# Six sums over the channels as two fp32r matmuls each, in the second mixer of a two-block network

## What is computed

```
qf = jax.nn.silu(q.astype(jnp.float32))
f = lower_bound + (1 - lower_bound) * jax.nn.sigmoid(f_logit.astype(jnp.float32))
kf = 1 - f
...
diff = b_[:, :, :, None, :] - b_[:, :, None, :, :]
decay = jnp.exp(jnp.where(causal[:, :, None], diff, -jnp.inf))
scores = jnp.einsum('bhtk,bhtsk,bhsk->bhts', q_, decay, k_)
o_intra = jnp.einsum('bhts,bhsv->bhtv', scores, v_)
```

## Time and profile before

| | |
|---|---|
| time, median of 3 runs (lowest to highest) | 1392.86 us (1390.56 to 1392.98) |
| the profiled execution's own time | 1392.87 us |
| its span | 1391.0 us |
| granted TensorE clock, mean | 0.999 of full speed |
| TensorE matmul (PE) busy | 1377.5 us, 99% |
| TensorE weight load (PEld) busy | 1147.1 us, 82% |
| VectorE (DVE) busy | 775.9 us, 56% |
| ScalarE (ACT) busy | 598.9 us, 43% |
| GpSimd (POOL) busy | 594.9 us, 43% |
| mean DMA rate | 105 GB/s |

### The profile page before, as it was taken

One profiled execution on the slowest core, in us unless ns is written; L12 is line 12 of the kernel. 1 busy time (PEld: TensorE's weight loads), 2 busy tenths in 40 slices (PEclk: granted clock), 3 DMA queues, 4 the chain that ended last, 5 costly groups with the idle time before them and its releaser, 6 DMA issues.

```text
span 1391.0 us, 20905 instructions
## 1 busy us (share of the span) xinstructions
PE 1377.5 (99%) x7666; PEld 1147.1 (82%) x7666; DVE 775.9 (56%) x1524; ACT 598.9 (43%) x1030; POOL 594.9 (43%) x314
## 2 busy tenths in 40 slices
PE   8999999999999999999999999999999999999998
PEld 7877777778998888888889978878898888888887
DVE  5897865456677666666884878522563323231222
ACT  7223555464255445443222525575354444342222
POOL 7432222216244444444543479523345444444441
PEclk9999999999999999999999999999999999999999
DMA  7931111015525444445662241121213233222321
GB/s 219 218 92 61 31 62 46 19 44 167 167 77 181 136 138 151 150 131 161 202 209 83 65 117 61 31 61 31 92 61 121 90 102 110 90 87 87 106 84 61
DMA packets 188309, 146.15 MB, mean 105 GB/s; under 512 B 21561, under 2 KB 186659, under 8 KB 188240
## 3 DMA queue, kind: packets, MB, share of 16 engines
q1 hardware_dynamic: 186528, 144.59, 33.9%
q10 hardware_dynamic: 1200, 0.36, 0.1%
q0 software_dynamic: 512, 0.25, 0.1%
HBM read 143.08 MB, written 2.10 MB: 104 GB/s over the span
## 4 chain that ended last, share of the span: by engine, by line
PE 91%; DVE 5%; DMA 2%; issue 1%; ACT 0%; DVEq 0%; ACTq 0%
PE ps L2120 27%; PE ps L2121 26%; PE ps L2122 26%; DMA ada<-in_ada_w 2%; DVE ps L1736 2%; PE ps L2564 2%; PE ps L2308 2%; PE ps L2391 1%; PE ps L2374 1%; PE ps L2621 1%; PE ps L2591 1%; PE ps L2644 1%; PE ps L2656 1%; PE ps L2206 0%; PE ps L2388 0%
## 5 line engine op out<-in xcount | busy, mean ns | idle before, releaser
L778 POOL TENSOR_TENSOR w_lo<-raw,w_hi 128x1024 fp32r<-128x1024 f32 (+2 forms) x224 | 515.5, 2305 | 726.4 <-ACT w_hi L843 448.5
L2120 PE MATMUL ps<-h_hi,w_hi 128*128 128x512 f32 (+1 forms) x1336 | 505.2, 378 | 0.6 <-DVE h_lo L1371 0.6
L2121 PE MATMUL ps<-h_lo,w_hi 128*128 128x512 f32 (+1 forms) x1336 | 494.3, 370 | 0.0
L2122 PE MATMUL ps<-h_hi,w_lo 128*128 128x512 f32 (+1 forms) x1336 | 494.2, 370 | 0.0
L2120 PEld LDWEIGHTS ps<-h_hi,w_hi 128*128 128x128 f32 x1336 | 252.3, 189 | 60.5 <-issue 17.7
L2122 PEld LDWEIGHTS ps<-h_hi,w_lo 128*128 128x128 f32 x1336 | 252.2, 189 | 43.2
L2121 PEld LDWEIGHTS ps<-h_lo,w_hi 128*128 128x128 f32 x1336 | 252.6, 189 | 39.9 <-issue 0.5
L843 ACT ACTIVATE w_hi<-raw 128x1024 fp32r<-128x1024 f32 (+2 forms) x136 | 133.6, 984 | 265.5 <-PE ps L2122 256.4
L1111 ACT ACTIVATE w_hi<-raw 128x1024 fp32r<-128x1024 f32 x88 | 93.2, 1059 | 218.0 <-PE ps L2122 218.0
L2120 PE MATMUL ps<-g_hi,w_hi 128*128 128x512 f32 (+1 forms) x394 | 146.8, 373 | 0.0
L2121 PE MATMUL ps<-g_lo,w_hi 128*128 128x512 f32 (+1 forms) x394 | 144.7, 367 | 0.0
(11 more groups left out here) (364 smaller groups left out, 1707.8 us busy)
## 6 DMA issues: line engine op xcount, KB each, us to landing
ada<-in_ada_w SPq DMA_DIRECT2D x48, 512.0 KB, 3.8
raw<-in_ffn_w_up SPq DMA_DIRECT2D x22, 1024.0 KB, 5.0
raw<-in_w_up SPq DMA_DIRECT2D x22, 1024.0 KB, 4.9
raw<-in_w_in SPq DMA_DIRECT2D x21, 1024.0 KB, 5.1
raw<-in_ffn_w_down SPq DMA_DIRECT2D x8, 896.0 KB, 5.7
raw<-in_w_down SPq DMA_DIRECT2D x8, 896.0 KB, 4.7
raw<-in_w_in SPq DMA_DIRECT2D x16, 256.0 KB, 3.8
raw<-in_w_out SPq DMA_DIRECT2D x4, 1024.0 KB, 5.1
```

The lines of the kernel that those rows point to most:

```text
L778: pool.tensor_tensor(w_lo[slot % 4][:, 0:nk, :], part[:, :, slot % 2 * P:(slot % 2 + 1) * P], w_hi[slot % 4][:, 0:nk, :].bitcast(F32), ALU ...
L2120: pe.matmul(out_ap, w, x, start=first, stop=False, **kw)
L2121: pe.matmul(out_ap, w, xl, start=False, stop=False, **kw)
L2122: return pe.matmul(out_ap, wl, x, start=False, stop=last, **kw)
```

## The change

The products of the summed chunks go to PSUM banks 4 and 5 in place of `hn`. ScalarE copies each to an fp32r tile, `sum_hi`; VectorE subtracts that from the product into `sum_lo`; TensorE sums both with the matrix of ones read as fp32r, one matmul after the other into the same bank. The semaphore of the low part takes the place of `multiplied` on TensorE. It and that of the high part are those which the first block's convolution used, under new names, counted on from 4 (`CC`). `sum_hi` lies in room behind `kd_odd` in the tile `off`, `sum_lo` where `hn` is.

```diff
+        sum_hi = sb("sum_hi", [P, 2, T], F32R, at=off_at + 4 * HG * T)
+        sum_lo = sb("sum_lo", [P, 2, T], F32R, at=hn_at)
+        PRODUCT_BANK = [4, 5]
...
                 hi(s + 4)
+                if S_QH + 2 < s < S_PAIRED:
+                    for c in ((0, 1), (2, 3), (4, 5))[s - S_KV2 + 1]:
+                        act.wait_ge(multiplied, c + 1)
+                        act.activation(sum_hi[:, c % 2, :], ps[PRODUCT_BANK[c % 2]][:, :], ACT.Copy).then_inc(split_hi_done, 1)
...
-                out = hn[:, c % 2, :]
+                out = ps[PRODUCT_BANK[c % 2]][:, :]
...
+            def product_lo(c):
+                dve.wait_ge(split_hi_done, CC + c + 1)
+                dve.tensor_tensor(sum_lo[:, c % 2, :], ps[PRODUCT_BANK[c % 2]][:, :], sum_hi[:, c % 2, :].bitcast(F32),
+                                  ALU.subtract).then_inc(split_lo_done, 1)
...
             scale_queries(0)
+            product_lo(0)
+            product_lo(1)
...
                     if c + 2 < SUMMED_CHUNKS:
                         multiply(c + 2)
+                for c in EARLY_CHUNKS[s]:
+                    if c + 2 < SUMMED_CHUNKS:
+                        product_lo(c + 2)
...
                 if c < SUMMED_CHUNKS:
-                    pe.wait_ge(multiplied, c + 1)
-                    ins = pe.matmul(bank[:, :], ones[:, :], hn[:, c % 2, :], start=True, stop=True)
+                    pe.wait_ge(split_lo_done, CC + c + 1)
+                    pe.matmul(bank[:, :], ones[:, :].bitcast(F32R), sum_hi[:, c % 2, :], start=True, stop=False)
+                    ins = pe.matmul(bank[:, :], ones[:, :].bitcast(F32R), sum_lo[:, c % 2, :], start=False, stop=True)
```

More of the change, by code:

```diff
@@ L199, in build @@
         sq = sb("sq", [P, 2, T])
+        hn_at = offset[0]
         hn = sb("hn", [P, 2, T])
@@ L333, in build @@
         pv_done, o_copied = sem("pv_done"), sem("o_copied")
-        tap_done, acc_added, ln_sum, ln_centred, ln_sq, ln_sqsum, ln_root, ln_norm, cv_ready, cv_hi_done, cv_lo_done = (
+        tap_done, acc_added, ln_sum, ln_centred, ln_sq, ln_sqsum, ln_root, ln_norm, cv_ready, split_hi_done, split_lo_done = (
             sem("tap_done"), sem("acc_added"), sem("ln_sum"), sem("ln_centred"), sem("ln_sq"), sem("ln_sqsum"), sem("ln_root"),
-            sem("ln_norm"), sem("cv_ready"), sem("cv_hi_done"), sem("cv_lo_done"))
+            sem("ln_norm"), sem("cv_ready"), sem("conv_and_sums_hi_done"), sem("conv_and_sums_lo_done"))
         att_hi_done, att_lo_done = sem("att_hi_done"), sem("att_lo_done")
@@ L1080, in _ @@
                 act.wait_ge(cv_ready, c + 1)
-                act.activation(cv_hi[:, c, :], acc[:, c, :], ACT.Copy).then_inc(cv_hi_done, 1)
+                act.activation(cv_hi[:, c, :], acc[:, c, :], ACT.Copy).then_inc(split_hi_done, 1)
                 hi(S_ATTN + 6 + c)
@@ L1697, in _ @@
             for c in range(CC):
-                dve.wait_ge(cv_hi_done, c + 1)
+                dve.wait_ge(split_hi_done, c + 1)
                 dve.tensor_tensor(cv_lo[:, c, :], acc[:, c, :], cv_hi[:, c, :].bitcast(F32),
-                                  ALU.subtract).then_inc(cv_lo_done, 1)
+                                  ALU.subtract).then_inc(split_lo_done, 1)
                 gated_attention(4 + c)
@@ L2414, in _ @@
             for s in range(S_CONV, S_OUT):
-                tile(s, cv_hi, cv_lo, ready=parts(cv_lo_done) if s == S_CONV else None)
+                tile(s, cv_hi, cv_lo, ready=parts(split_lo_done) if s == S_CONV else None)
             def ada_tile(n, buf, count):
```

## The result

| | before | after |
|---|---|---|
| time, median of 20 runs each (lowest to highest) | 1393.13 us (1390.56 to 1395.13) | 1390.21 us (1387.77 to 1392.58) |
| the profiled execution's own time | 1392.87 us | 1389.30 us |
| its span | 1391.0 us | 1387.6 us |
| matmul (PE) busy | 1377.5 us | 1374.2 us |
| VectorE (DVE) busy | 775.9 us | 780.2 us |

The ratio after to before is 0.9981, with a 95% interval of 0.9976 to 0.9987: 1.8 to 3.3 us less. 1.6 us were forecast (1391.3 us, range 1389.5 to 1393.3), from a median of three runs that lay 0.3 us lower.

A forecast was written before the change was run, and what follows sets the result against it. TensorE's matmuls were taken to bound the kernel (under way for 99% of the span), unless TensorE then waits for VectorE and GpSimd. 2.42 - 0.48 - 0.35 = 1.6 us saved, giving 1391.3 us, range 1389.5 to 1393.3.

The forecast's parts named there:

- TensorE's own saving: Six fp32 sums, 5.14 us, become twelve fp32r matmuls, 2.72 us: 2.42 us saved, 0.81 a pair.
- Chunks 0 and 1: First pair of sums: subtractions end near 819.5, TensorE wants them at 820.82, so no wait, 1.3 us spare.
- Chunks 2 and 3: Second pair of sums: chunk 3's product, still held by GpSimd's `kd_odd`, makes TensorE wait; 0.48 us lost.
- Chunks 4 and 5: Third pair of sums: no TensorE wait, but `merge_decays(0)` 0.28 us later; 1.94 us saved at the attention's first products.
- Steps 0 to 2: Attention steps: `merge_decays(1)` gets its turn one `lo` sooner, step 1's scores end near 846.0; just fits.
- The rival in which VectorE stays: Steps 0 to 2: `merge_decays(1)` waits for the next `lo` as before; 0 to 0.6 us remains, 1392.6 us; chance 0.19.
- Chunk 10: Level 3's queries and keys both end near 857.9, chunk 10 starts near 858.1; 0.35 us lost, 1.6 left.
- all of it is kept: Rival: both half-microsecond waits, at chunk 3 and chunk 10, are absent; 1390.45 us; chance 0.18.
- the likeliest case: The forecast itself, 1.6 us saved, 1391.3 us, own range 1390.7 to 1392.0; chance 0.52.
- Slower by a turn: Rival at level 3: `scale_queries(3)` loses one more turn, ends at 861.4; 1.9 us slower, 1394.8 us; chance 0.07.
- No fp32r rate: Rival at the sums: twelve matmuls cost 0.857 us each, as in fp32; 5.1 us more, 1398 us; chance 0.02.

The follow-up runs named there:

- run 9: Changed kernel with `kd_odd` behind chunk 3's product, GpSimd's low weights a level later, chunk 6's scores behind step 1's; ratio to before 0.9983, median 1389.82 us.
- Run 2: Changed kernel with the products kept in `hn` in SBUF instead of PSUM; one execution, 1393.60 us, lead -2.20 us after chunk 10.
- run 3: Changed kernel with GpSimd's first `kd_odd` made to wait for the product of chunk 3; ratio to before 0.9970, 1388.98 us.
- run 7: Changed kernel with the edits of run 3 and run 6 together; ratio to before 0.9986, 1390.58 us.
- run 6: Changed kernel with GpSimd's low weights of tiles 140 and 141 each made one level later; one execution, 1391.44 us, lead 1.95 us after chunk 10.

## Why the prediction was right, point by point

- **TensorE's own saving, 2.42 us.** Right, and 0.11 us too small. The pairs cost 0.91 us, and run 9, where nothing waits, keeps 2.53. The other 0.1 lies in the tiles behind the first two pairs, 0.05 in each: tile 135 took 5.50 us behind the fp32 sums (822.53, where they end, to 828.03) and takes 5.44 behind the new ones (821.60 to 827.04), because the first matmuls behind an fp32 sum start about 0.232 us apart (seven steps from 822.76 to 824.39).
- **Chunks 0 and 1, no wait.** Right: the subtractions end at 819.2, 1.5 us before TensorE wants them. Run 2 shows that this hung on the operand in PSUM: held by GpSimd, they start chunk 1 2.5 us later (8.39 us behind tile 134's start in place of 5.90), and a stretch at the lower clock follows.
- **Chunks 2 and 3, 0.48 us lost.** Right in place and cause, 0.61 measured: 0.56 up to the next tile, and 0.05 in that tile, whose first matmuls start about 0.232 us apart, as they do behind an fp32 sum. The product of chunk 3 took 2.69 us with its output in PSUM, so the place of the output frees nothing; run 3 took `kd_odd` out of its way and the wait went. Chunk 3 itself started at 828.11 on the clock of the kernel before (0.13 is added from here on to times of the changed kernel), where 828.15 was forecast. What the count left out is that a stalled pair does not run at 0.227 us: its second matmul starts 0.30 behind the first (827.98 to 828.28).
- **Chunks 4 and 5, VectorE 0.28 us later.** Right in kind: `merge_decays(0)` starts at 831.80, which is 831.93 on the clock of the kernel before, 0.41 later. The lead at step 0 is 1.91 against 1.94.
- **Steps 0 to 2, VectorE comes forward by one turn.** Right. `merge_decays(1)` was there at 838.1 (837.8 by the count), went ahead of the second `lo`, and step 1's scores ended at 846.16 (846.0). TensorE passed with the lead unchanged at 1.93. The rival in which VectorE stays would have shown 0 to 0.6. How tight it is appears in run 7: 0.6 us more lead, and 0.32 of it is lost at that very place.
- **Chunk 10, 0.35 us lost.** Right in place, but mis-sized: 0.14 measured, 0.06 at its start and 0.08 within it. `kd_odd` ended at 857.67, not 857.9, and chunk 10 started 0.15 behind that, not 0.2. The queries were not the limit: `scale_queries(3)` ended at 855.44, where the count had both near 857.9. VectorE had waited 1.38 us for GpSimd's `hg` and took the turn at 850.92, 0.05 us ahead of the next `lo`; run 6, with one `lo` less ahead of level 3, shows that the wait hangs on that queue.
- **The end.** Forecast lead 1.6, measured 1.79 on the chain of matmuls: 2.53 - 0.61 - 0.13. That it came so near is in part luck, since the saving (0.11 too small) and the wait at chunk 3 (0.13 too small) nearly cancel, and what is left is the 0.22 us of chunk 10. The median moved by 2.9 in the first comparison, of which 1.8 is the change; 0.4 can be the mean clock of the runs, and for the rest the runs show no cause beyond their scatter. By the median alone (1390.21) the rival "all of it is kept" (1390.45) would have fitted better than the forecast, and 1390.21 lies outside the likeliest case's own 1390.7 to 1392.0; only the starts in the trace tell the two apart. The chances had 0.82 for less than 0.2%, and it was 0.19% by that comparison.
- **The rivals.** All kept: did not happen, but run 9 shows that it can, with three edits that take away three waits. Slower by a turn: in both profiles of the changed kernel `scale_queries(3)` got its turn, at 855.44 in the first, 4.3 us ahead of the 859.7 from which that rival decides. No fp32r rate: ruled out by 0.227 us a matmul.

## What to carry to other kernels

When the engine that sets the end gets 2 us less to do, list what it takes from the others over the next steps and how much room each has; here the rows of before named four such places, and the saving was cut at two of them, by 0.61 and 0.13 us. Work on a helper engine can be free while it is behind cover and still be what stops the next saving: the added twelve instructions cost 0.01 us with the old matmuls, and with the new ones the waits for VectorE and GpSimd take 0.7 of 2.5 us. A change of 2 us in 1390 is read to 0.03 us from one profile by the starts of two matmuls; 20 runs of each kernel told that there is a gain, but not whether it is 1.8 or 3.3. Fix the zero right ahead of the change and look whether the difference still stands 100 us on.

## What the runs showed of the hardware

- A VectorE instruction with two tensors in SBUF and a GpSimd instruction that reads SBUF exclude each other for their whole length and take turns, the one that waits coming next, in the rows of this stretch: 2.69 us for a product of 0.69, wherever its output goes; 5.65 us for two subtractions with both operands in SBUF, 1.27 with one in PSUM, 1.47 with both in SBUF and GpSimd idle.
- Behind the one wait of 2.04 us the granted clock was 0.51 for 3.5 us, and the matmuls cost 0.427 us in place of 0.227. The waits of 0.3 to 0.7 us in the other runs had no such stretch behind them, nor had one of 0.97 us for VectorE at 729 us in the changed kernel. One profile does not show that the wait was the cause.
- Behind fp32 sums, and behind a stalled pair, the next fp32r matmuls of 512 columns start about 0.232 us apart in place of 0.227, which costs 0.05 us in a tile.
- A stretch at the lower clock, 3.4 us long, came behind the matmuls of one column in 7 of 12 profiles, at the same place of the program, and cost 1.3 to 1.6 us each time.
